# Expert routing of a two-layer block: scratch rows in PSUM, a separate bank for the turned places, and per-tile waits of the first expert

## The reference, cut to what matters

```python
def expert_choice_moe(h, w_router, w_gate, w_up, w_down):
    b, n, d = h.shape
    cap = EC_FACTOR * n // N_EXPERTS
    aff = jax.nn.softmax(jnp.einsum('bnd,de->bne', h, w_router).astype(jnp.float32), axis=-1)
    g, idx = lax.top_k(jnp.swapaxes(aff, 1, 2), cap)
    xs = jax.vmap(lambda hb, ib: hb[ib])(h, idx)
    hid = jax.nn.silu(jnp.einsum('becd,edf->becf', xs, w_gate)) * jnp.einsum('becd,edf->becf', xs, w_up)
    y = jnp.einsum('becf,efd->becd', hid, w_down) * g[..., None].astype(h.dtype)
    return jax.vmap(lambda yb, ib: jnp.zeros((n, d), h.dtype).at[ib.reshape(-1)].add(yb.reshape(-1, d)))(y, idx)
```

## Time and profile before

| | |
|---|---|
| median of 3 runs | 2829.12 us |
| lowest, highest run | 2822.04, 2836.18 us |
| span of the profiled execution | 2829.2 us |
| PE busy | 2600.4 us (92%) |
| DVE busy | 1692.6 us (60%) |
| ACT busy | 903.5 us (32%) |
| POOL busy | 222.1 us (8%) |
| HBM read | 524.85 MB |
| routing of layer 0, from its first MAX8 to the first expert's matmul | 2164.15 to 2194.30 us |
| routing of layer 1, the same | 2586.34 to 2605.26 us |

### The profile page before, as it was taken

How to read it: one execution, slowest core, us unless ns; L and a number is a source line. 1 busy time by engine, 2 the same in 40 slices (tenths; PEclk the granted TensorE clock), 3 DMA queues, 4 the chain that set the end, 5 groups by cost and what they waited for, 6 DMA issues and landing times. The chain is left out here.

```text
span 2829.2 us, 38297 instructions
## 1 busy us (share of the span) xinstructions
PE 2600.4 (92%) x14442; PEld 1908.1 (67%) x14442; DVE 1692.6 (60%) x2549; ACT 903.5 (32%) x1489; POOL 222.1 (8%) x372
## 2 busy tenths in 40 slices
PE   5999999998999999999999878997988999798988
PEld 4888887665887888887887558995666333566322
DVE  4876785444787778877778557785533233563101
ACT  2222235443422223422225444445333100443100
POOL 0010121321001100011010000000002000000000
PEclk9999998998999999999999989998989999888998
DMA  7665552332256756557654116763114899416997
GB/s 277 194 197 179 169 169 75 75 75 77 77 183 198 246 171 185 151 168 229 201 187 100 45 57 197 218 180 104 45 43 174 365 428 424 116 38 264 419 427 338
DMA packets 428865, 528.09 MB, mean 187 GB/s; under 512 B 29766, under 2 KB 382532, under 8 KB 416292
## 3 DMA queue, kind: packets, MB, share of 16 engines
q1 hardware_dynamic: 392592, 399.52, 41.2%
q0 software_dynamic: 35520, 126.24, 14.0%
q10 hardware_dynamic: 596, 0.19, 0.0%
HBM read 524.85 MB, written 1.05 MB: 186 GB/s over the span
## 5 line engine op out<-in xcount | busy, mean ns | idle before, releaser
L2095 DVE TENSOR_TENSOR wlo<-raw,whi 128x1024 fp32r<-128x1024 f32 x392 | 476.2, 1222 | 186.8 <-ACT whi L1546 177.6
L1546 ACT ACTIVATE whi<-raw 128x1024 fp32r<-128x1024 f32 x392 | 413.0, 1057 | 516.6 <-PE bank L699 487.8
L697 PE MATMUL bank<-xhi,whi 128*128 128x512 f32 (+1 forms) x1560 | 569.6, 365 | 5.2 <-DVE xlo L2731 2.9
L698 PE MATMUL bank<-xlo,whi 128*128 128x512 f32 (+1 forms) x1560 | 561.7, 360 | 0.0
L699 PE MATMUL bank<-xhi,wlo 128*128 128x512 f32 (+1 forms) x1560 | 561.3, 360 | 0.0
L2134 DVE SCALAR_TENSOR_TENSOR acc<-mod_ring,conds,acc 128x1024 f32<-128x1024 f32 x336 | 415.9, 1278 | 11.6 <-DMA mod_ring<-in_w_ada 5.5
L697 PEld LDWEIGHTS bank<-xhi,whi 128*128 128x128 f32 x1560 | 295.8, 190 | 62.9 <-issue 20.4
L699 PEld LDWEIGHTS bank<-xhi,wlo 128*128 128x128 f32 x1560 | 295.7, 190 | 44.7
L698 PEld LDWEIGHTS bank<-xlo,whi 128*128 128x128 f32 x1560 | 295.9, 190 | 42.7 <-issue 0.7
L697 PE MATMUL bank<-hhi,whi 128*128 128x512 f32 (+1 forms) x764 | 268.9, 352 | 0.0
L699 PE MATMUL bank<-hhi,wlo 128*128 128x512 f32 (+1 forms) x764 | 266.2, 348 | 0.0
(11 more groups left out here) (335 smaller groups left out, 3510.8 us busy)
## 6 DMA issues: line engine op xcount, KB each, us to landing
raw<-in_ffn_w_in SPq DMA_DIRECT2D x176, 512.0 KB, 4.4
mod_ring<-in_w_mod POOLq DMA_DIRECT2D x128, 512.0 KB, 4.5
experts<-in_w_gate SPq DMA_DIRECT2D x32, 2048.0 KB, 21.0
experts<-in_w_up SPq DMA_DIRECT2D x32, 2048.0 KB, 20.6
experts<-in_w_down SPq DMA_DIRECT2D x32, 2048.0 KB, 21.0
mod_ring<-in_w_ada POOLq DMA_DIRECT2D x96, 512.0 KB, 4.8
raw<-in_ffn_w_out SPq DMA_DIRECT2D x64, 384.0 KB, 4.0
raw<-in_ffn_w_out SPq DMA_DIRECT2D x64, 320.0 KB, 3.6
```

Source lines behind the costliest of these rows:

```text
L697: pe.matmul(o, wh, hi[:, k0 + k, cols], start=(first and k == 0), stop=False)
L698: pe.matmul(o, wh, lo[:, k0 + k, cols], start=False, stop=False)
L1546: act.activation(whi[:, slot, :], raw[:, slot, :], ACT.Copy).then_inc(*n.mark("hi_ready"))
L2095: dve.tensor_tensor(wlo[:, slot, :], raw[:, slot, :], whi[:, slot, :].bitcast(F32), ALU.subtract)\
```

## The change

The mask and the working row of the selection (`taken`, `work`) become the two halves of `bank[3]`, in all four rounds; `place` stays in `tmp`. The places are turned into `bank[2]` instead of `bank[4]`, with a semaphore of its own (`place_turned`), so bank 4 is free from the first MATCH_REPLACE8 on. The four waits for banks 4 to 7 after the gathers are taken out; in their place the first expert's `gate_up` waits, before the two matmuls of each j, for the bank of gather (g, j) to be read: 16 waits in layer 0 and 8 in layer 1.

```diff
--- before.py
+++ after.py
@@ -232,7 +232,7 @@
     + [f"st_done{g}" for g in range(2)]
     + [f"sums_done{c}" for c in range(T // P)]
     + [f"square_sum{c}" for c in range(T // P)]
-    + ["consts_in", "consts_made", "root_made", "token_hi", "tokens_split", "place_ready", "oh_ready", "ohw_ready"]
+    + ["consts_in", "consts_made", "root_made", "token_hi", "tokens_split", "place_ready", "place_turned", "oh_ready", "ohw_ready"]
 )
 
 
@@ -1371,16 +1371,20 @@
                 for i in range(3, 2 * len(tts)):
                     turn_tokens(i)
                 pe.wait_ge(*n.next("place_ready"))
-                acquire(4)
+                acquire(2)
                 rows = 32 * groups
                 for t in range(2):
-                    mm = pe.transpose(bank[4][:, t * 64:t * 64 + rows], tmp[0:rows, 2, t * P:(t + 1) * P], tab("ident")[0:rows, 0:rows])
-                mm.then_inc(s["bank_ready4"], 1)
+                    mm = pe.transpose(bank[2][:, t * 64:t * 64 + rows], tmp[0:rows, 2, t * P:(t + 1) * P], tab("ident")[0:rows, 0:rows])
+                mm.then_inc(s["place_turned"], 1)
                 n.next("token_hi", 3)
+                placed = {}
 
                 def gather(g, k):
 
-                    small_product(gather_bank(g, k, groups), [(x[:, k, 2 * g + t, :], oh[:, 2 * g + t, :, :]) for t in range(2) for x in token_parts[l][0:2]])
+                    b = gather_bank(g, k, groups)
+                    acquire(b)
+                    small_product(b, [(x[:, k, 2 * g + t, :], oh[:, 2 * g + t, :, :]) for t in range(2) for x in token_parts[l][0:2]], acq=False)
+                    placed[g, k] = n.peek(f"bank_read{b}:free", 1)
 
                 for g in range(groups):
                     pe.wait_ge(*n.next("tokens_split", 4))
@@ -1390,8 +1394,6 @@
                 for k in range(2, KD):
                     for g in range(groups):
                         gather(g, k)
-                for b in range(4, 8):
-                    evacuated(b)
 
                 def turn_places():
 
@@ -1418,6 +1420,8 @@
                         pe.wait_ge(*expert_full(l, p, (kind, i)))
                         slots.append(expert_slot(l, p, (kind, i))[1])
                     for j in range(KD):
+                        for g in range(groups if p + i == 0 else 0):
+                            pe.wait_ge(*placed[g, j])
                         for part, done in enumerate(("gate_used", "up_used")):
                             mm = pe.matmul(bank[i][part * HD:part * HD + ns, :], gathered[l][:, j, 2 * p + i, 0:ns],
                                            experts[slots[part]][:, j * 512:(j + 1) * 512],
@@ -2002,7 +2006,8 @@
                 own()
                 for b in range(5, 8):
                     act.sem_inc(s[f"bank_read{b}"], len(range(b - 5, 2 * nt, 3)))
-                n.next("bank_read4", 2)
+                n.next("bank_read4")
+                n.next("bank_read2")
                 for k in range(KD):
                     banks = [gather_bank(g, k, nt // 2) for g in range(nt // 2)]
                     if k % 2:
@@ -2763,7 +2768,7 @@
                 dve.tensor_tensor(A, A, total.unsqueeze(2).broadcast_to([P, nt, N_EXP]), ALU.mult).then_inc(*n.mark("softmax_in"))
 
                 rows = slice(0, 32 * groups)
-                work, place, taken = (tmp[rows, i, LAT] for i in (1, 2, 3))
+                work, place, taken = bank[3][rows, LAT], tmp[rows, 2, LAT], bank[3][rows, CTX]
                 dve.wait_ge(*n.filled(4))
                 for i in range(CAP // 8):
                     source = work if i else bank[4][rows, LAT]
@@ -2778,14 +2783,14 @@
                     .then_inc(*n.mark("dve"))
                 own()
                 dve.tensor_tensor(place, place, taken, ALU.mult).then_inc(*n.mark("place_ready"))
-                dve.wait_ge(*n.filled(4))
+                dve.wait_ge(*n.next("place_turned"))
                 own()
                 for tt in tts:
                     at0 = tt % 2 * 64 + tt // 2 * 32
-                    dve.tensor_tensor(oh[:, tt, :, :], bank[4][:, at0:at0 + N_EXP].unsqueeze(2).broadcast_to([P, N_EXP, CAP]),
+                    dve.tensor_tensor(oh[:, tt, :, :], bank[2][:, at0:at0 + N_EXP].unsqueeze(2).broadcast_to([P, N_EXP, CAP]),
                                       tab("slots").unsqueeze(1).broadcast_to([P, N_EXP, CAP]), ALU.is_equal).then_inc(*n.mark("oh_ready"))
                 own()
-                dve.sem_inc(*n.mark("bank_read4"))
+                dve.sem_inc(*n.mark("bank_read2"))
                 for i in range(2 * nt):
                     n.next(f"bank_read{5 + i % 3}")
                 for k in range(KD):
```

## The result

| | before | after |
|---|---|---|
| median | 2829.12 us | 2815.59 us |
| lowest, highest of 5 runs | 2822.04, 2836.18 | 2811.13, 2820.59 |
| ratio | | 0.995, interval 0.9929 to 0.997 |
| span of the profiled execution | 2829.2 us | 2809.9 us |
| mean granted clock in it | 0.956 | 0.963 |

The change makes the kernel 13.5 us faster (by the interval 8.5 to 20), where 7.4 us were forecast. The time lies in the range of the forecast, but the excess of 6 us is nearly as large as the forecast itself, so it needs a cause of its own.

The account below looks back on a forecast made before the run. Bound: the routings' chain through DVE's selection, turn of places, `oh`, gathers and the wait after. Gains 3.9, 1.0, 1.9, 1.2 less 0.1 (PSUM), 0.4 (clock), 0.1 (waits) make 7.4 us: 2829.2 to 2821.8 us, range 2813 to 2830.

Parts of the forecast that it names:

- Scratch rows in PSUM: Both routings, DVE's selection: three instructions no longer held up beside POOL, gaining 2.64 us in layer 0, 0.88 in layer 1.
- whose operands are all in SBUF: DVE's selection in the routings: such an instruction is held up about 0.9 to 1.0 us while POOL works on SBUF.
- DVE stays held up: Rival, DVE's selection: one SBUF operand beside POOL suffices for the delay; only bank and waits gain, 2824.7 us; chance 0.08.
- A bank of their own: Start of gathers: needs only its group's two `oh`; 1.24 us sooner in layer 0, 0.13 of the hop in each layer.
- The clock inside the gathers: Gathers, both layers: full clock may return a little earlier or later against their start; 0.4 us taken as lost.
- a sign of failure: Gathers: the forecast fails if full clock comes later behind their start than 3.2 us (layer 0) and 3.9 (layer 1).
- The waits: Before the first expert: tile-by-tile waits close the gaps, gaining 1.9 and 1.2 us; the added waits cost 0.1.
- The stream follows: Expert weights: DMA resumes when the first `gate_up` frees a ring slot, so an earlier first expert starts the stream earlier.
- The sum: Whole kernel: gains and costs in both routings come to 7.4 us, from 2829.2 to 2821.8 us.
- each microsecond of lead should reach the end: From the first expert to the kernel's end, both layers: PE's later stalls move with the stream, so lead is kept.
- The range: Whole kernel: 2813 to 2830 us, holding the forecast and first three rivals, with scatter of the runs the larger part.
- the change stays within 14 us: Whole kernel: the difference stays within about 0.5%, 14 us, what a measurement can tell from no change; chance 0.90.

## Why the prediction was right, point by point

- **Scratch rows in PSUM: right.** Foreseen were 0.45, 0.69 and 0.42 us beside a running L2965; they took 0.42, 0.68 and 0.41. PSUM cost MATCH_REPLACE8 0.41 instead of 0.40 us, and MAX8 nothing (0.42). The table of the Trainium skill (page "VectorE: DVE Perf Modes", section "The TRN2 errata — SBUF-src ops pay a fixed extra latency per instruction") has 58 cycles of fixed cost from SBUF to SBUF and 120 from PSUM to SBUF, by which each of them would have cost an estimated 0.065 us more; this trace doesn't show it. The reading that an instruction "whose operands are all in SBUF" is held up was too simple, since MAX8 and MATCH_REPLACE8 had theirs there too, as the prediction itself notes. And the rival "DVE stays held up" left out that L2775 has no operand in SBUF after the change; with its 0.79 and 0.88 us the rival would have stood at 2823.0 instead of 2824.7 us.
- **A bank of their own: right.** The gathers start 7.56 us behind the first MAX8 instead of 11.36, 3.8 sooner for 3.9 foreseen; in layer 1 7.38 instead of 8.34, 0.96 for 1.0. POOL was in time for the second group.
- **The clock inside the gathers: right in size, but a sign of failure came.** They take 17.06 and 9.89 us, where it was 16.93 and 9.45: 0.57 us lost, 0.4 foreseen. Full clock comes back later behind their start than before, 3.5 us instead of 3.2 in layer 0 and 4.8 instead of 3.9 in layer 1, which the prediction had named as a sign that it fails. It cost what the term had allowed and no more: layer 1's lead is 1.72 us where 2.2 were foreseen. The windows of after in which it returns, to be read against the earlier trace rows:

```profile
2171.00:2172.00 1.00, 1.00 (x4) 0.75 (x3) 0.00 (x0) 0.00 (x0) 1.00 (x2) 0.55 0.96 410
2581.00:2582.00 1.00, 1.00 (x5) 0.75 (x4) 0.07 (x1) 0.23 (x1) 0.00 (x0) 0.76 0.96 410
```

  With the scratch rows alone the loss was 1.7 us of 3.4.
- **The waits: right.** The gaps of 1.86 and 1.13 us are gone wholly (the first matmul now starts 0.07 us before the shown end of the gathers), 1.93 and 1.20 for 1.9 and 1.2. The first `gate_up`, up to ACT's read of its bank, takes 7.22 instead of 7.19 us.
- **The stream follows: right.** The windows of after, which answer to the earlier trace rows, show it resume in the ten us behind the first `gate_up`:

```profile
2180.00:2190.00 10.00, 10.00 (x46) 5.66 (x46) 3.00 (x4) 4.38 (x6) 0.00 (x0) 1.00 0.00 0
2190.00:2200.00 10.00, 10.00 (x60) 3.85 (x58) 0.69 (x1) 1.15 (x2) 0.00 (x0) 1.00 0.67 257
```

  PE's first long wait in the chain for weights is 21.53 us long, at 2297.41, 8.91 earlier than in the earlier trace rows, and the first expert came 8.94 earlier. Up to the table load early in layer 1 the changed kernel then took 0.68 us longer (table above).
- **The sum: 7.4 us foreseen in the routings, 7.3 found there.** But the step "so each microsecond of lead should reach the end" was incomplete. I asked what the stages behind do with an earlier start, and looked at the weight stream alone. The clock was priced only inside the gathers. The same question, asked of layer 1's attention, where the windows of before show 0.79, would have shown some 9 us that a shift can set free or take. What came out beyond the lead is about 6, by the medians, and how much of it lies there is not shown. It would not have told the sign.
- **The range: in part luck.** The terms alone allowed 2819 to 2825 us, and 2815.6 lies outside. The range of 2813 to 2830 held it because it was widened for the scatter of the executions, not for a gain in clock further down, which the prediction does not have. The statement that the change stays within 14 us held by a hair: 13.5 us by the medians, 14.1 by the ratio.

## What to carry to other kernels

An instruction that takes two or three times as long in one layer as in another, with the same shape, may be held up by something that runs beside it: look at what the other engines do at that moment, and try one operand in the other memory. A wait for all tiles in front of a loop over tiles can go into the loop at no visible cost on PE, if the loop is slower than the filling of the tiles. And where stretches of low PE activity follow behind a change, the clock there can come out differently by as much time as the change itself brings (here 89.0 to 97.8 us for the same work), so the stage that was changed has to be measured in the trace, and the median needs an A/A comparison and variants with pure delay before a gain is put down to the edit.

## What the runs showed of the hardware

- VectorE with source and destination in PSUM: TENSOR_SCALAR of 64x256 float32 0.42 us, MATCH_REPLACE8 0.41.
- VectorE with both inputs in SBUF beside a GpSimd instruction on SBUF: a scan 1.64 instead of 0.68 us, TENSOR_TENSOR 1.30 instead of 0.41; with one of the inputs in PSUM, no delay (DVE's timelines above). This agrees with the Trainium skill, page "SBUF — State Buffer", section "Who interferes with whom", by which a VectorE instruction with two SBUF inputs contends with a GpSimd instruction that reads SBUF, and one with at most one SBUF input does not, outside VectorE's two-port modes.
- TENSOR_SCALAR with its one input in SBUF was held up beside GpSimd all the same: 1.24 and 1.33 us, against 0.42 with source and destination in PSUM. MAX8 and MATCH_REPLACE8 with one input in SBUF were not (0.42 and 0.40 us). Which mode the TENSOR_SCALAR ran in, no run shows.
- Sixteen satisfied waits between the 32 matmuls of `gate_up`: 0.03 us in all.
- A matmul of 128x512 from plain float32 operands: 0.88 us at full clock; from fp32r operands 0.24.
- Identical work of 553 matmuls took 89.0 to 97.8 us, and its length went with the granted clock, 1.00 to 0.90.
